# Delta layer: the neighbours' bias written to its scratch during the inverse, two square sums behind tile six, the eighth square sum and its copy one tile later

## The chip, the cores and the metric

The kernel runs on one core of a Trainium2 chip. The metric is the device time of one execution in microseconds. The kernel before takes 2214.55 us, the median of three runs.

The engines are called by their roles here: TensorE (PE in the profile) multiplies matrices, VectorE (DVE) and ScalarE (ACT) work element by element, GpSimd (POOL) does a few element-wise steps and issues some transfers, SyncE (SP) issues most of the transfers. Each engine works through its own instructions in order, and the engines wait for one another by semaphores.

## What is computed

The reference runs two blocks of two layers each over 256 tokens of width 1024. The change lies in the very first layer, a gated delta rule:

```python
def gdn_mixer(x, w_in, conv_w, a_log, dt_bias, norm_w, w_o):
    proj = x @ w_in
    qkv = jax.nn.silu(causal_depthwise_conv(proj[..., :3 * hk], conv_w))
    q = l2_normalize(qkv[..., :hk].reshape(shp)) * (GDN_HEAD_DIM ** -0.5)
    k = l2_normalize(qkv[..., hk:2 * hk].reshape(shp))
    v = qkv[..., 2 * hk:3 * hk].reshape(shp)
    ...
    o = gated_delta_rule_chunked(q, k, v, g, beta)
    o = rms_norm(o, norm_w) * jax.nn.silu(z)
    return o.reshape(b, t, hk).astype(x.dtype) @ w_o
```

`l2_normalize` divides by the root of the sum of squares over each head's 128 columns, for 8 heads of q and 8 of k. `gated_delta_rule_chunked` solves with a unit lower triangular matrix per chunk and head; the kernel inverts it.

The neighbourhood attention of the second block adds a bias `rpb` to its scores, which depends on the distance of two grid cells. That bias is a small input (8 heads, 2 layers). The kernel spreads it into a scratch in device memory early on and reads it back in the second block, from 1070 us on.

## The kernel before

**The projection by tiles.** `gdn_layer` works on x (turned, so that channels lie on the partitions). The weight `gdn_w_in` comes in 16 panels of 1 MB through a ring of three buffers, loaded by SyncE (`load_panel`, line 433); the buffer of a panel is free for the third next one when the panel has been split. For each panel ScalarE makes a rounded high half (`lin.high`, line 2153) and VectorE the rest as a low half (`lin.low`, line 2166), and there are two buffers for the halves. A panel holds two tiles of 128 output columns, so there are 32 tiles (GDN_OUT). TensorE makes each tile of 24 products (lines 355 to 357: 8 parts of the sum by three products of halves) of 256 tokens, into PSUM banks 0 to 2 in turn. Tiles 0 to 7 are q, 8 to 15 k, 16 to 23 v, 24 to 31 the gate z.

**What follows a tile.** ScalarE copies tile t out with the last tap of the convolution (`evict`, line 2505), VectorE adds the other three taps from PSUM (`conv`, line 2668), ScalarE applies the silu (line 2511) and, for q and k, squares the result (line 2517) into one of four buffers. TensorE sums a square over the partitions by a product with a matrix of ones (`square_sum`, line 2373): sums 0 and 1 go to the halves of bank 3, 2 and 3 to bank 4, 4 and 5 to bank 3 and so on. ScalarE copies a pair of sums out (`sums_out`, line 2540).

**What sets the order.** Everything is written out by hand in each engine's block, in loops over t. In TensorE's loop, the list `summed_behind` says which square sums come behind which tile; without an entry it is sum t - 5 behind tile t. Sum 0 waits also for D_ROWS, which VectorE raises at the end of `rows()` (last instruction at line 2694), a step behind the convolution of tile 4 that reads banks 3 to 7 for the decay. In ScalarE's loop, silu and square of tile t - 2 stand behind `evict(t)`, except that at t = 9, 10, 11 the exponentials of the decay stand there, and at t = 12, 13, 14 two silus with their squares. Square t (from 4 on) waits for sum t - 4, whose buffer it takes. A sum with an even number from 4 on waits for the copy of the pair before the last. In ScalarE's loop `sums_out` of pair p stands at t = 2p + 7. The high halves of the next panel are made at the start of `evict(t)` for even t, as soon as tile t - 1 has been multiplied; the low halves stand in VectorE's loop ahead of `conv(t)` for even t. In VectorE's loop two masks of the decay follow `conv(6)` and `conv(8)`.

**GpSimd.** It clears `pad` (line 2299), loads the neighbours' bias into it by 16 small transfers (line 2057), waits for them, and issues two transfers (line 2061) that write each layer's rows 64 times over into `rpb_dram`, 1792 KB each. Later it multiplies by beta, and during the inverse it makes the left factors of the products: `pair[lev % 2][t]` for levels 1 to 5 and the two chunks t (line 2316), each 128x1024. Its last instruction in the layer is the wait for the two stores.

**The inverse.** Six levels (LEVELS). At each level and for each chunk TensorE multiplies `pair` with X, ScalarE copies the product out, TensorE makes two more products, and VectorE subtracts them from X and its transpose (lines 2792 and 2794). TensorE waits for GpSimd's `pair` of the level by `ready`. In between VectorE also makes low halves of the output weight, behind level 1.

Of the kernel before, what the change touches and what calls it, by code (L numbers as in the profile page):

```python
# [42 lines left out]
ROWS = SEQ // GRID_W  # L43
# [2002 lines left out]
    dve_n.passed(6)  # L2046


def store_rpb(pr, pool, pad):


    i = pr.ins
    n_rows, at = 2 * ROWS - 1, GRID_W - WIN_COLS
    pool.wait_ge(pr.table_set.sem, pr.table_set.at(1))
    for l in range(DEPTH):
        for h in range(8):
            pool.dma_start(pad[h * n_rows:(h + 1) * n_rows, l, at:at + 2 * WIN_COLS - 1],
                           i["rpb_b_2"][l, h, WIN_ROWS - ROWS:WIN_ROWS + ROWS - 1, :]).then_inc(pr.rpb_in.sem, 16)
    pool.wait_ge(pr.rpb_in.sem, pr.rpb_in.at(16 * 8 * DEPTH))
    for l in range(DEPTH):  # L2060
        pool.dma_start(pr.rpb_dram[l].rearrange("c r x -> r c x"),
                       pad[:, l, :].unsqueeze(1).to_broadcast([8 * n_rows, GRID_W, P])).then_inc(pr.rpb_out.sem, 16)
# [145 lines left out]
def gdn_layer(pr, hand):  # L2208
# [12 lines left out]
    with ExitStack() as ctx:  # L2221
# [33 lines left out]
        pad = pr.sb(ctx, "rpb_rows", [8 * (2 * ROWS - 1), DEPTH, P])  # L2255
# [12 lines left out]
        with nc.Block() as block:  # L2268
# [27 lines left out]
            @block.gpsimd  # L2296
            def _(pool):
                pool.wait_ge(pr.taken_dve.sem, by_dve(0))
                pool.memset(pad[:, :, :], 0.0).then_inc(pr.table_set.sem, 1)
                store_rpb(pr, pool, pad)  # L2300

                pool.wait_ge(load.sem, load.at(80))
                pool.wait_ge(act_n.sem, act_n.at(A_DECAY))
                pool.wait_ge(pr.taken_dve.sem, by_dve(GDN_V + 1))
                for t in range(2):
                    pool.tensor_tensor(A[:, t], A[:, t], beta[:, t, :].unsqueeze(2).to_broadcast([P, H, P]), ALU.mult).then_inc(ready.sem, 1)
                for lev in range(1, LEVELS):
                    for t in range(2):
                        if lev == 1 and t == 0:
                            pool.wait_ge(ss_mm.sem, ss_mm.at(GDN_V))  # L2310
                        if lev == 1:
                            pool.wait_ge(dve_n.sem, dve_n.at(D_V))
                            pool.wait_ge(act_n.sem, act_n.at(A_AT + t))
                        else:
                            inv[t].begin(pool, 4 * (lev - 2) + 1)
                        pool.tensor_tensor(pair[lev % 2][t], AT[:, t], pr.const(f"pairT{2 << lev}").unsqueeze(1).to_broadcast([P, H, P]), ALU.mult).then_inc(ready.sem, 1)
                pool.wait_ge(pr.rpb_out.sem, pr.rpb_out.at(32))

            @block.tensor
            def _(pe):  # L2320
# [76 lines left out]
                            mm = pe.transpose(bank(K_BANKS[h // 4])[:, h % 4, :], k[:, h, chunk[0]], ident)  # L2397
                    mm.then_inc(pe_n.sem, 1)

                summed_behind = {12: [], 13: [7], 14: [8, 9], 15: [10, 11], 16: [12], 17: []}  # L2400
                pe.wait_ge(pr.ones_set.sem, pr.ones_set.at(2))
                for _ in range(10):
                    pe.matmul(ps[:, 2, 0:P], pr.full_ones, pr.full_ones, start=True, stop=True)
# [91 lines left out]
            def _(act):  # L2495
# [23 lines left out]
                def small():  # L2519
                    act.wait_ge(dve_n.sem, dve_n.at(D_LOGIT))  # L2520
                    act.activation(rate, par[:, 0, :], ACT.Exp)
                    act.activation(beta, ab[:, :, H:2 * H], ACT.Tanh, scale=0.5)
                    do(act.activation(soft, neg_abs, ACT.Exp))
                    act.activation(soft, soft, ACT.Ln, bias=1.0).then_inc(act_n.sem, 1)
# [13 lines left out]
                def sums_out(p):  # L2538
                    act.wait_ge(ss_mm.sem, ss_mm.at(2 * p + 2))
                    act.activation(sums[:, 2 * p:2 * p + 2, :].rearrange("p n c -> p (n c)"), ps[:, 3 + p % 2, :], ACT.Copy).then_inc(ss_out.sem, 1)  # L2540
# [29 lines left out]
                for t in range(GDN_OUT):  # L2570
                    evict(t)
                    if t == 0:
                        act.wait_ge(pe_n.sem, pe_n.at(P_AB))
                        act.activation(ab[:, :, :], ps[:, 3, 0:32].rearrange("p (t c) -> p t c", t=2), ACT.Copy).then_inc(act_n.sem, 1)
                        small()
                    if t in (9, 10, 11):
                        decay(t - 9)
                    elif t in (12, 13, 14):
                        silu(2 * t - 17)
                        silu(2 * t - 16)  # L2580
                    elif 2 <= t < 22:
                        silu(t - 2)
                    if t >= 7 and t % 2 and t <= 21:
                        sums_out((t - 7) // 2)
                    if t in (21, 22):
                        log(t - 21)
                    if t in (23, 25):
                        lin.high(act, lin.next_panel(t + 1))
                    if t in (23, 24):
                        root(t - 23)  # L2590
                    if t in (25, 26):
                        silu(2 * t - 30)
                        silu(2 * t - 29)
# [1506 lines left out]
```

## Time and profile before

| | us |
|---|---|
| runs of the kernel before | 2213.85, 2214.55, 2215.47 |
| median | 2214.55 |
| span of the profiled execution | 2222.0 |
| TensorE busy in it | 2150.3 |
| VectorE busy | 1610.9 |
| ScalarE busy | 1194.4 |
| GpSimd busy | 163.1 |

The span goes from the first to the last instruction of one profiled execution; it is 7.45 us longer than the median of the plain runs. A row of the timeline gives the start and the length of a group of like instructions in us, then engine, line, operation, what is written and read, the count, and in brackets how long the engine stood idle before it and what released it. Times count from the start of the span.

### The profile page before, as it was taken

Reading aid. Unit: us, or ns where it says so; the run is one execution under the profiler, and the core shown is the slowest. Engines: PE = TensorE matmul, PEld = TensorE weight load, DVE = VectorE, ACT = ScalarE, POOL = GpSimd, SP = SyncE. Lnnn points to the kernel's source line nnn. Section 1 sums busy time; section 2 is a strip of 40 time slices with the busy share of each in tenths; the row PEclk is TensorE's granted clock in tenths of the full one; section 3 lists DMA queues with packets and bytes.
Section 4 is the critical chain, followed back from the end, with each engine's and each line's share of the span. In section 5 each row is a group of like instructions: output and inputs, shape, how many; then the busy total and the mean of one; then the engine's idle time right before and its main releaser. Section 6 shows DMA issues by size and latency. Waiting matters only on the chain.

```text
span 2222.0 us, 39694 instructions
## 1 busy us (share of the span) xinstructions
PE 2150.3 (97%) x16153; PEld 1987.7 (89%) x16153; DVE 1610.9 (72%) x2318; ACT 1194.4 (54%) x1701; POOL 163.1 (7%) x182
## 2 busy tenths in 40 slices
PE   9999999999899998999999999999999999999998
PEld 8988788888678887999988999999999988899997
DVE  6775788855688887777767667777877876757664
ACT  5855577655667766333566545333433456545433
POOL 2140000002000000000510001000000410001000
PEclk9999999999999999999999999999999999999999
DMA  8522499874149993555632345555555653346552
GB/s 227 181 78 78 178 337 336 307 207 144 39 161 355 339 338 116 180 176 177 178 114 95 99 149 190 171 170 170 172 178 177 177 155 114 115 152 218 171 197 87
DMA packets 258570, 400.20 MB, mean 180 GB/s; under 512 B 17081, under 2 KB 204338, under 8 KB 258418
## 3 DMA queue, kind: packets, MB, share of 16 engines
q1 hardware_dynamic: 253138, 383.83, 51.4%
q0 software_dynamic: 5168, 14.17, 2.7%
q8 instruction: 111, 1.82, 0.3%
q14 instruction: 41, 0.34, 0.1%
q10 hardware_dynamic: 112, 0.05, 0.0%
HBM read 390.15 MB, written 7.86 MB: 179 GB/s over the span
## 4 chain that ended last, share of the span: by engine, by line
PE 52%; DVE 4%; ACT 2%; DMA 2%; issue 1%; DVEq 0%; ACTq 0%
PE psum_banks L355 15%; PE psum_banks L357 15%; PE psum_banks L356 15%; DMA weight_ring<-w_in 2%; DVE weights_low L780 1%; PE psum_banks L3538 1%; PE psum_banks L364 1%; PE psum_banks L365 1%; PE psum_banks L366 1%; ACT weights_high L2153 1%; PE psum_banks L3544 1%; PE psum_banks L3563 1%; DVE source_low L633 1%; PE psum_banks L3573 0%; PE psum_banks L3604 0%
## 5 line engine op out<-in xcount | busy, mean ns | idle before, releaser
L355 PE MATMUL psum_banks<-source_high,weights_high 128*128 128x272 f32 (+1 forms) x2336 | 680.5, 291 | 8.8 <-DVE hidden L795 3.7
L357 PE MATMUL psum_banks<-source_high,weights_low 128*128 128x272 f32 (+1 forms) x2336 | 671.0, 287 | 0.0
L356 PE MATMUL psum_banks<-source_low,weights_high 128*128 128x272 f32 (+1 forms) x2336 | 670.1, 287 | 0.0
L355 PEld LDWEIGHTS psum_banks<-source_high,weights_high 128*128 128x128 f32 x2336 | 442.2, 189 | 14.6 <-issue 7.2
L356 PEld LDWEIGHTS psum_banks<-source_low,weights_high 128*128 128x128 f32 x2336 | 442.6, 189 | 0.9
L357 PEld LDWEIGHTS psum_banks<-source_high,weights_low 128*128 128x128 f32 x2336 | 442.0, 189 | 0.0
L780 DVE TENSOR_TENSOR weights_low<-weight_ring,weights_high 128x2048 fp32r<-128x2048 f32 x131 | 293.1, 2290 | 94.9 <-ACT weights_high L774 94.8
L774 ACT ACTIVATE weights_high<-weight_ring 128x2048 fp32r<-128x2048 f32 x131 | 242.1, 1910 | 179.8 <-PE psum_banks L357 138.3
L2166 DVE TENSOR_TENSOR weights_low<-weight_ring,weights_high 128x2048 fp32r<-128x2048 f32 x96 | 223.0, 2323 | 145.1 <-ACT weights_high L2153 144.6
L2153 ACT ACTIVATE weights_high<-weight_ring 128x2048 fp32r<-128x2048 f32 x95 | 181.3, 1908 | 27.3 <-PE psum_banks L357 19.4
L785 ACT ACTIVATE silu_gate<-silu_gate 128x272 f32<-128x272 f32 (+1 forms) x88 | 37.7, 428 | 271.8 <-DVE silu_gate L794 271.8
L1804 DVE TENSOR_TENSOR weights_low<-weight_ring,weights_high 128x2048 fp32r<-128x2048 f32 x70 | 160.3, 2291 | 22.9 <-ACT weights_high L1581 22.4
L355 PE MATMUL psum_banks<-hidden_high,weights_high 128*128 128x272 f32 x528 | 153.3, 290 | 0.3 <-DVE h L808 0.3
L357 PE MATMUL psum_banks<-hidden_high,weights_low 128*128 128x272 f32 x528 | 152.4, 289 | 0.0
L356 PE MATMUL psum_banks<-hidden_low,weights_high 128*128 128x272 f32 x528 | 151.8, 287 | 0.0
L1581 ACT ACTIVATE weights_high<-weight_ring 128x2048 fp32r<-128x2048 f32 x70 | 133.7, 1914 | 26.6 <-PE psum_banks L366 21.4
L808 DVE SCALAR_TENSOR_TENSOR h<-psum_banks,h 128x272 f32<-128x272 f32 x264 | 107.8, 437 | 32.9 <-PE psum_banks L357 31.4
L1804 DVE TENSOR_TENSOR weights_low<-more_ring,weights_high 128x2048 fp32r<-128x2048 f32 x50 | 114.5, 2290 | 14.9 <-ACT weights_high L1581 14.6
L364 PE MATMUL psum_banks<-weights_high,hidden_high 128*128 128x512 f32 x256 | 102.2, 399 | 6.0 <-DVE weights_low L1804 2.7
L621 POOL TENSOR_TENSOR normed<-normed 128x272 f32<-128x272 f32 (+1 forms) x35 | 35.9, 1026 | 971.9 <-ACT normed L613 969.4
L1581 ACT ACTIVATE weights_high<-more_ring 128x2048 fp32r<-128x2048 f32 x50 | 95.6, 1912 | 19.0 <-PE psum_banks L366 17.5
L364 PE MATMUL psum_banks<-weights_high,slots 128*128 128x512 f32 (+1 forms) x256 | 99.3, 388 | 1.6 <-issue 0.9
(541 smaller groups left out, 4392.7 us busy)
## 6 DMA issues: line engine op xcount, KB each, us to landing
weight_ring<-ffn_w_in SPq DMA_DIRECT2D x88, 1024.0 KB, 6.7
weight_ring<-w_in SPq DMA_DIRECT2D x48, 1024.0 KB, 5.2
weight_ring<-ffn_w_out SPq DMA_DIRECT2D x44, 1024.0 KB, 5.0
weight_ring<-moe_w_down SPq DMA_DIRECT2D x24, 1024.0 KB, 6.6
weight_ring<-moe_w_gate SPq DMA_DIRECT2D x44, 512.0 KB, 4.8
weight_ring<-moe_w_up SPq DMA_DIRECT2D x44, 512.0 KB, 6.4
weight_ring<-gdn_w_in SPq DMA_DIRECT2D x16, 1024.0 KB, 6.0
more_ring<-moe_w_gate SPq DMA_DIRECT2D x32, 512.0 KB, 5.2
```

Source lines behind the costliest of these rows:

```text
L355: pe.matmul(out, w_hi, x_hi, start=start, stop=False)
L356: pe.matmul(out, w_hi, x_lo, start=False, stop=False)
L357: return pe.matmul(out, w_lo, x_hi, start=False, stop=stop)
L364: pe.matmul(out, x_hi, w_hi, start=start, stop=False)
L774: act.activation(split_at(par, part)[0], pr.ring[:, n % RING, :], ACT.Copy).then_inc(hi_n.sem, 1)
L780: dve.tensor_tensor(lo, pr.ring[:, n % RING, :], hi.bitcast(F32), ALU.subtract).then_inc(lo_n.sem, 1)
L785: act.activation(silu[:, m, toks], silu[:, m, toks], ACT.Silu).then_inc(sd.sem, 1)
L808: dve.scalar_tensor_tensor(h[:, j, toks], ps[:, 4 + j % 4, toks], 0.5, h[:, j, toks], ALU.mult, ALU.add).then_inc(ad.sem, 1)
L1581: act.activation(split_at(s)[0], ring_at(u, part), ACT.Copy).then_inc(hi_n.sem, 1)
L1804: dve.tensor_tensor(lo, ring_at(u, part), hi.bitcast(F32), ALU.subtract).then_inc(lo_n.sem, 1)
L2153: act.activation(self.hi[:, p % self.slots, :], self.pr.ring[:, n % RING, :], ACT.Copy).then_inc(self.pr.split_hi.sem, 1)
L2166: dve.tensor_tensor(self.lo[:, p % self.slots, :], self.pr.ring[:, n % RING, :], self.hi[:, p % self.slots, :].bitcast(F32), ALU.subtract) ...
```

## The change

The function that loads the neighbours' bias and writes it to its scratch is cut in two. The loads stay where they were. The wait for them and the two stores go into GpSimd's loop over the levels of the inverse, behind both chunks' products for level 2 and ahead of those for level 3. GpSimd's wait for the end of the stores stays the last of the layer.

In TensorE's list the square sums 0 and 1 both go behind tile 6 (they were behind tiles 5 and 6), and sum 7 goes behind tile 14 (it was behind 13), so that tile 14 is followed by sums 7, 8 and 9. In ScalarE's loop the copy of sums 6 and 7 goes from t = 13 to t = 14, behind the two silus and squares of that turn.

```diff
-def store_rpb(pr, pool, pad):
+def load_rpb(pr, pool, pad):
 
 
     i = pr.ins
@@ -2056,6 +2056,11 @@
         for h in range(8):
             pool.dma_start(pad[h * n_rows:(h + 1) * n_rows, l, at:at + 2 * WIN_COLS - 1],
                            i["rpb_b_2"][l, h, WIN_ROWS - ROWS:WIN_ROWS + ROWS - 1, :]).then_inc(pr.rpb_in.sem, 16)
+
+
+def store_rpb(pr, pool, pad):
+
+    n_rows = 2 * ROWS - 1
     pool.wait_ge(pr.rpb_in.sem, pr.rpb_in.at(16 * 8 * DEPTH))
     for l in range(DEPTH):
         pool.dma_start(pr.rpb_dram[l].rearrange("c r x -> r c x"),
@@ -2297,7 +2302,7 @@
                 pool.memset(pad[:, :, :], 0.0).then_inc(pr.table_set.sem, 1)
-                store_rpb(pr, pool, pad)
+                load_rpb(pr, pool, pad)
@@ -2314,6 +2319,8 @@
                         pool.tensor_tensor(pair[lev % 2][t], AT[:, t], pr.const(f"pairT{2 << lev}").unsqueeze(1).to_broadcast([P, H, P]), ALU.mult).then_inc(ready.sem, 1)
+                    if lev == 2:
+                        store_rpb(pr, pool, pad)
                 pool.wait_ge(pr.rpb_out.sem, pr.rpb_out.at(32))
@@ -2397,7 +2404,7 @@
-                summed_behind = {12: [], 13: [7], 14: [8, 9], 15: [10, 11], 16: [12], 17: []}
+                summed_behind = {5: [], 6: [0, 1], 12: [], 13: [], 14: [7, 8, 9], 15: [10, 11], 16: [12], 17: []}
@@ -2580,8 +2587,10 @@
-                    if t >= 7 and t % 2 and t <= 21:
+                    if t >= 7 and t % 2 and t <= 21 and t != 13:
                         sums_out((t - 7) // 2)
+                    if t == 14:
+                        sums_out(3)
```

## Rows read from the trace of the kernel before

**Rows 1.** The page, section 1: busy us, share of the span, instructions.

```profile
PE 2150.3 (97%) x16153; PEld 1987.7 (89%) x16153; DVE 1610.9 (72%) x2318; ACT 1194.4 (54%) x1701; POOL 163.1 (7%) x182
```

**Rows 2.** Waits of TensorE, 0 to 140 us: us in total, times, longest.

```profile
PE psum_banks L2373 <- DVE decay_small L2694: 2.5, 1, 2.5
PE psum_banks L355 <- DVE weights_low L2166: 2.2, 1, 2.2
...
PE psum_banks L2373 <- ACT squares L2517: 0.8, 1, 0.8
```

**Rows 3.** Timeline of TensorE: first products of tiles 6 and 7.

```profile
42.41 0.47 PE L355 MATMUL psum_banks<-slots,weights_high 128*128 128x256 f32 x1
...
45.71 0.47 PE L355 MATMUL psum_banks<-slots,weights_high 128*128 128x256 f32 x1
```

**Rows 4.** Timeline, 69 to 79 us: tiles 14 and 15, square 12, sums 10 and 11.

```profile
69.00 2.29 DVE L2166 TENSOR_TENSOR weights_low<-weight_ring,weights_high 128x2048 fp32r<-128x2048 f32 x1 [1.47 <-ACT weights_high L2153]
...
71.91 0.47 PE L355 MATMUL psum_banks<-slots,weights_high 128*128 128x256 f32 x1
...
75.64 0.47 PE L355 MATMUL psum_banks<-slots,weights_high 128*128 128x256 f32 x1
...
77.89 0.42 ACT L2517 ACTIVATE squares<-qkv 128x256 f32<-128x256 f32 x1
...
78.70 1.03 PE L2373 MATMUL psum_banks<-squares,full_ones 128*128 128x256 f32 x4
```

**Rows 5.** Windows: length, busy PE, PEld, DVE, ACT, POOL; clock, DMA share, GB/s.

```profile
74.90:140.00 65.10, 64.63 (x530) 63.48 (x529) 50.58 (x52) 43.50 (x60) 5.80 (x2) 1.00 0.43 137
```

**Rows 6.** Timeline, 46 to 56 us: VectorE ahead of tile 10, and tile 10.

```profile
46.18 1.52 DVE L2668 SCALAR_TENSOR_TENSOR qkv<-psum_banks,conv_w,qkv 128x253 f32<-128x253 f32 x3 [0.60 <-ACT qkv L2505]
...
49.81 1.51 DVE L2668 SCALAR_TENSOR_TENSOR qkv<-psum_banks,conv_w,qkv 128x253 f32<-128x253 f32 x3
52.52 2.29 DVE L2166 TENSOR_TENSOR weights_low<-weight_ring,weights_high 128x2048 fp32r<-128x2048 f32 x1 [1.20 <-ACT weights_high L2153]
...
55.61 0.47 PE L355 MATMUL psum_banks<-slots,weights_high 128*128 128x256 f32 x1
```

**Rows 7.** Line 2061, the two stores: ns min/median/max, first and last start.

```profile
L2061 POOL DMA_DIRECT2D rpb_scratch<-rpb_rows x2: 1680/1710/1741, 30.5 to 32.2; - x2
...
DMA to landing us min/median/max: 16.4/21.9/27.3
```

**Rows 8.** Line 433, the only weight load issued between 35 and 45.5 us.

```profile
L433 SPq DMA_DIRECT2D weight_ring<-gdn_w_in x1: 368/368/368, 35.2 to 35.2; - x1
...
DMA to landing us min/median/max: 25.2/25.2/25.2
```

**Rows 9.** Transfers issued from 0 to 230 us: KB each, median us to landing.

```profile
weight_ring<-gdn_w_in SPq DMA_DIRECT2D x16, 1024.0 KB, 6.0
```

**Rows 10.** Timeline, 60 to 65 us: halves for tile 12, and tile 12.

```profile
60.44 1.91 ACT L2153 ACTIVATE weights_high<-weight_ring 128x2048 fp32r<-128x2048 f32 x1 [1.36 <-DMA weight_ring<-gdn_w_in]
...
62.39 2.29 DVE L2166 TENSOR_TENSOR weights_low<-weight_ring,weights_high 128x2048 fp32r<-128x2048 f32 x1 [2.52 <-ACT weights_high L2153]
...
64.73 0.39 PE L355 MATMUL psum_banks<-slots,weights_high 128*128 128x256 f32 x1 [2.17 <-DVE weights_low L2166]
```

**Rows 11.** Timeline of the inverse, 153 to 177 us.

```profile
153.11 2.35 POOL L2316 TENSOR_TENSOR squares<-a_turned,consts_gdn 128x1024 f32<-128x1024 f32 x1
...
155.64 4.28 DVE L2166 TENSOR_TENSOR weights_low<-weight_ring,weights_high 128x2048 fp32r<-128x2048 f32 x1
...
161.53 1.15 PE L2425 MATMUL psum_banks<-inverse_pair,squares 64*64 64x64 f32 x32 [0.98 <-DVE inverse_pair L2794]
...
163.09 1.15 PE L2425 MATMUL psum_banks<-inverse_pair,spare_pair 64*64 64x64 f32 x32 [0.41 <-DVE inverse_pair L2794]
...
176.29 1.95 PE L2326 MATMUL psum_banks<-inverse_pair,spare_pair 128*128 128x128 f32 x16
```

**Rows 12.** The core: span, and mean granted clock of TensorE.

```profile
core 0: 2222.0 us, clock 0.990
```

## Prediction

> **What bounds the kernel now.** I began with the page's busy shares: TensorE is busy for 97% of the span [rows 1], so the time falls only where TensorE stands idle. The change touches the first 200 of 2222 us, so I went next to what TensorE waits for in the first 140 us. Three waits lie in the changed region: 2.5 us at a square sum (line 2373) for VectorE's line 2694, 2.2 us at a tile for the low halves of its weights (line 2166), and 0.8 us at a square sum for ScalarE's square (line 2517) [rows 2]. Then I read the order of time around each. A wait names only the engine that came last, so the reader must look there for what would have come next. The same rows give the unit prices: a tile of 24 products takes 3.30 us from its first product to that of the next tile when one square sum lies behind it (42.41 to 45.71 [rows 3]), and 3.73 us with two (71.91 to 75.64 [rows 4]). So one more sum costs 0.43 us, and a tile without any takes 2.87. From 74.9 to 140 us TensorE is busy for 64.63 of 65.10 us at the full clock [rows 5]: what is won before is carried through that stretch, and nothing is to be won in it. A difference under 0.2% (4.4 us) is about what a measurement of this kernel can't tell from no change.
>
> **Part 1, the first two sums behind tile 6.** Now sum 0 stands behind tile 5 and holds TensorE for 2.5 us [rows 2], because VectorE is still making the decay rows out of the banks that the sum overwrites; tile 6 starts at 42.41 [rows 3]. With the sum behind tile 6, tile 6 starts at once and ends near 42.5, when the decay rows are done. The two sums follow, the number of sums stays the same, and tile 7 stands at 45.71 - 2.5 = 43.2 us. ScalarE's square 4 needs sum 0 for its buffer, but it comes after the copy of tile 6, which is later than the sum: nothing. What is late next is VectorE's queue. It has 0.60 us of idle before the convolution at 46.18. Without that idle it starts this convolution at 45.58, needs 3.63 us to the start of the next (46.18 to 49.81, the mask lies between), 1.45 for that one, and begins the low halves for tile 10 at 50.66 where it began them at 52.52; they last 2.29 us, to 52.95 [rows 6]. Tile 10 stood at 55.61 [rows 6]; less 2.5 is 53.1. It just fits, with 0.15 us to spare. Part 1 gives 2.5 us; if VectorE's queue is longer by more than the spare, the excess is lost.
>
> **Part 2, the scratch written later.** The two stores of 1792 KB each start at 30.5 and 32.2 us and take 16.4 and 27.3 us to land [rows 7]. In that time SyncE issues the load of one weight panel at 35.2 us, which lands 25.2 us later, at 60.4 [rows 8]; the median of the 16 such loads is 6.0 us [rows 9]. ScalarE waits 1.36 us for it before the high halves at 60.44, the low halves follow at 62.39, and tile 12 starts at 64.73 after 2.17 us of idle [rows 10]. Without the wait ScalarE would come to it at 59.08, and with part 1 at 56.6. A load of 6 us from 35.2 is there at 41, with 15 us to spare. So the 1.36 us goes entirely and tile 12 stands at 64.73 - 2.5 - 1.36 = 60.87. The other 0.8 us of the idle stays: it is ScalarE's own queue (the exponentials of the decay stand in it). Part 2 gives 1.36 here, not 2.17.
>
> Where the stores go, GpSimd issues for 2 x 1.71 = 3.42 us [rows 7] after the second level's products, so its third-level products begin at 156.5 instead of 153.11 (times of before; all shifts alike) [rows 11]. Behind them are queued those of levels four and five, and TensorE waits for each. VectorE's low halves at 155.64 take 4.28 us, against 2.29 elsewhere [rows 6, 11]: they stood behind a GpSimd product. That makes VectorE late, and TensorE idles 0.98 us before 161.53 and 0.41 before 163.09 [rows 11]. With GpSimd busy issuing instead, VectorE starts at once and is done at 157.93; two third-level products of 2.35 us each [rows 11] then end at 160.3 and 162.6. TensorE starts the first at about 160.5 and the second at 162.7 instead of 163.09: a gain of 0.4 us, with GpSimd last. The next two pairs end at 167.3 and 172.0; TensorE came to the second half of level five at 176.29, so 6.6 us per level, and to that of level four near 169.7 [rows 11]: time to spare in both. Bounds for the inverse: 0.9 us gained, if GpSimd is never last, and 3.4 lost, if its whole issue time reaches TensorE. I take 0.4, where the rows put it. The landing is hidden: from 156.6 it may take 27.3 us again, to 184, and behind the product at 176.29 the rest of level five, the state products and the output part are still to come before GpSimd's last wait matters.
>
> The Trainium skill (SBUF — State Buffer, "SBUF: two separate sides") says that VectorE and GpSimd share one port pair as an exclusive lock, held by the first to start for its whole instruction; a VectorE instruction with two SBUF inputs takes part in it against a GpSimd one that reads SBUF. By that rule, the trace agrees: 4.28 us [rows 11]. The same section warns that GpSimd can't write a transfer's descriptors while VectorE holds the pair in its faster modes; applied to these low halves the second issue would stretch to the end of them, which is the first price of rival C.
>
> **Part 3, the eighth sum and its copy a tile later.** Sum 7 waits 0.8 us behind tile 13 [rows 2], but tile 14 needs low halves that are made from 69.00 for 2.29 us. It could have started at 71.34 where it started at 71.91 [rows 4]. So the wait is worth 0.57 us only, and one sum goes behind tile 14 for 0.43. Tile 14 stands 3.86 + 0.57 = 4.4 us sooner, tile 15 only 4.4 - 0.43 = 4.0: net 0.1. The copy (line 2540) now comes behind square 12, and sum 10 must await it, as it overwrites the same bank. Square 12 starts at 77.89 and lasts 0.42; ScalarE comes to it 3.86 + 0.48 us sooner (the copy no longer lies ahead), so it ends at 73.97 and the copy, 0.6 at most, by 74.55. Sum 10 stood at 78.70 [rows 4]; less 4.0 is 74.7. It fits, again by 0.15 us. Bounds 0 and 0.6 us, the copy's length; I take 0.
>
> **The sum.** 2.5 + 1.36 + 0.1 + 0.4 = 4.4 us. The profiled execution's span is 2222.0 us, 7.45 over the median of the runs. The stretches in question run at full clock and nothing in them would scale the difference, so 4.4 comes off both: 2217.6 for the span, 2214.55 - 4.4 = 2210.2 for the median. Behind the layer nothing is changed. The mean granted clock of 0.990 [rows 12] says that some short stretches run at 1.2 GHz; a shift of 4 us may add or remove part of one. I bound this at 1.5 us either way, an estimate.
>
> **Rivals.** A, the forecast: 2210.2 (2209.0 to 2211.3), chance 0.58. B, a thin margin fails: VectorE's queue at tile 10 or the copy ahead of sum 10 comes late. For it: both margins are 0.15 us, and a semaphore between two engines takes a part of that. Against it: the queues are back to back in the rows already. Price 0.6 to 1.9 us, so 2210.8 to 2212.1; chance 0.16. C, GpSimd's issues become the wait in the inverse. It is last already in my sum. If VectorE's low halves hold the second issue to 157.93, the pair ends at 161.2 and 163.6, 0.9 us worse than A; if the whole 3.42 reaches TensorE, 3.8 worse: 2211.1 to 2214.0, chance 0.12. Against it: the two issues of now lasted 1.68 and 1.74 us [rows 7], though such low halves ran beside the second. D, slower than before: the stores now fill the transfer engines while TensorE runs the inverse, hundreds of products in few us, whose instructions must themselves be loaded by transfers. If one such load is held as the panel was, 25.2 against 6.0, so by up to 19 us [rows 8, 9], the kernel is slower by over 0.2% from the point where 8.8 us of it meet TensorE: 2219 to 2229. Against it: the same stores lay beside tiles 3 to 10, and there no wait of TensorE is without a named releaser [rows 2]. Chance 0.05. E, more than the forecast: the 0.8 us before tile 12 and all of the inverse's 0.9 fall too, or a slow clock stretch goes: 2206.5 to 2209, chance 0.09. That the change does nothing would need the load at 35.2 to be late for another reason and VectorE to stay last at tile 7; the rows leave no room for both.
>
> **How the numbers follow.** The line at 0.2% is 2214.55 - 4.43 = 2210.1, in the middle of A. 0.37 of A lies below it; with E that is 0.46 for faster. The rest of A, B and C make 0.49 for the same, D 0.05 for slower. The range goes from inside E, 2207.3, to 2213.0, most of C; what it leaves out is D and the ends of C and E.
>
> **What would show it.** Right: no wait at line 2373 before 80 us; the load near 35 us lands in under 10; one wait of 0.8 us at tile 12; the low halves in the inverse last 2.3 us; tile 15 stands 4.0 us sooner. Wrong: a wait for line 2166 at tile 10, for line 2540 behind tile 15, for GpSimd's line 2316 well over 0.1 us, or TensorE idle with no releaser while the stores land.

## The result, and the profile after

The changed kernel takes 2230.31 us (median of 11 runs, 2225.66 to 2237.27), where the kernel before takes 2217.77 beside it (11 runs, 2213.85 to 2228.44; the three known before the prediction were among the lowest). The ratio is 1.0054, with a 95% interval from 1.0041 to 1.0067: about 12 us slower, where 4.4 us less were forecast. The profiled execution has a span of 2226.9 us, 4.9 more than before.

First, the waits of TensorE from 0 to 140 us, as in [rows 2] (us in total, times, longest):

```profile
PE psum_banks L2410 <- DVE full_ones L2742: 1.9, 1, 1.9
PE psum_banks L355 <- DVE weights_low L2171: 1.3, 2, 0.7
PE psum_banks L2432 <- issue: 0.4, 1, 0.4
```

Both waits at the square sums are gone (line 2373 is 2380 now). The low halves (2166, now 2171) are waited for twice: 0.7 us at tile 12 and 0.6 at tile 14. The weight load issued near 35 us lands in 6 us, against the 25.2 of [rows 8]:

```profile
L433 SPq DMA_DIRECT2D weight_ring<-gdn_w_in x1: 368/368/368, 36.1 to 36.1; - x1
...
DMA to landing us min/median/max: 6.1/6.1/6.1
```

So far it went as written. The waits of TensorE from 130 to 200 us show where the time went:

```profile
PE psum_banks L2432 <- DVE inverse_pair L2803: 8.4, 4, 6.8
PE psum_banks L2432 <- issue: 4.6, 2, 4.3
```

In the kernel before, the first was 3.5 us in total, with none over 1.0, and the second 0.4. A wait that the profile puts down to "issue" is one without a named releaser. The timeline of the inverse, which answers to [rows 11], shows both in their places (start, length, engine, line, what, idle before):

```profile
149.56 3.48 POOL L2066 DMA_DIRECT2D rpb_scratch<-rpb_rows  x2
...
152.11 10.07 DVE L2171 TENSOR_TENSOR weights_low<-weight_ring,weights_high 128x2048 fp32r<-128x2048 f32 x1
...
153.03 2.40 POOL L2321 TENSOR_TENSOR squares<-a_turned,consts_gdn 128x1024 f32<-128x1024 f32 x1
...
155.35 2.38 POOL L2321 TENSOR_TENSOR spare_pair<-a_turned,consts_gdn 128x1024 f32<-128x1024 f32 x1
...
157.66 6.72 POOL L2321 TENSOR_TENSOR temp<-a_turned,consts_gdn 128x1024 f32<-128x1024 f32 x2
...
163.79 1.97 PE L2432 MATMUL psum_banks<-inverse_pair,squares 64*64 64x64 f32 x32 [6.78 <-DVE inverse_pair L2803]
...
173.96 0.26 PE L2432 MATMUL psum_banks<-inverse_pair,a_strict 64*64 64x64 f32 x1 [4.25 <-issue]
```

VectorE's low halves last 10.07 us. They are asked for at 152.11, while GpSimd issues, and end at 162.18. GpSimd's products go ahead of them: two of 2.4 us, untouched, and one of the next pair. The fourth waits for VectorE. Until then VectorE can't subtract level 2, and TensorE idles 6.78 us. At 169.7 TensorE stops again, for 4.25 us in the middle of a group of 32 equal products, and no engine is named. And the clock falls. The windows (length, busy PE, PEld, DVE, ACT, POOL, then granted clock, DMA share, GB/s):

```profile
158.00:162.00 4.00, 0.00 (x0) 0.00 (x0) 4.00 (x1) 0.00 (x0) 4.00 (x2) 0.92 1.00 190
162.00:166.00 4.00, 2.21 (x42) 2.21 (x44) 3.20 (x9) 0.13 (x1) 2.52 (x2) 0.50 0.98 177
166.00:170.00 4.00, 3.71 (x91) 3.57 (x89) 0.00 (x0) 1.92 (x2) 4.00 (x2) 0.73 0.88 164
170.00:174.00 4.00, 0.04 (x2) 0.04 (x2) 0.00 (x0) 0.00 (x0) 0.52 (x1) 0.70 0.93 207
174.00:178.00 4.00, 4.00 (x77) 4.00 (x78) 1.82 (x5) 0.00 (x0) 0.00 (x0) 0.50 0.55 165
```

With each of the two stops the clock goes to 0.50, its 1.2 GHz level, for a while, and 32 products take about 1.7 us instead of 0.93. The transfer engines are 88 to 100% busy from 158 to 174 us.

The first product behind the inverse (line 2453, now 2460) is the mark by which all runs can be compared. It starts at 182.69 us in the kernel before and here at

```profile
192.50 2.02 PE L2460 MATMUL psum_banks<-v_tokens,inverse_pair 128*128 128x128 f32 x16 [0.87 <-DVE inverse_pair L2807]
```

which is 9.8 us later. But 0.9 us of that arose ahead of everything that was changed. From 16 to 25 us TensorE works without a pause in every trace. In most of them part of that stretch is at the 1.2 GHz level, and how much differs between executions of the same code. The windows (columns as above) of the kernel before, of the changed kernel, and of the run below in which SyncE issues the stores:

```profile
16.00:25.00 9.00, 9.00 (x64) 8.82 (x65) 4.91 (x9) 3.93 (x10) 4.81 (x10) 0.81 0.78 244
```

```profile
16.00:25.00 9.00, 9.00 (x51) 8.68 (x51) 3.85 (x8) 2.83 (x8) 5.45 (x11) 0.62 0.77 238
```

```profile
16.00:25.00 9.00, 9.00 (x76) 8.83 (x76) 6.33 (x17) 4.29 (x8) 5.27 (x11) 1.00 0.76 240
```

So the mark alone can be off by up to 3 us, and what a change did is better read from ScalarE's copy of tile 4 on, which stands ahead of the first moved sum. It starts at 36.72 us in the kernel before and at 37.63 here:

```profile
36.72 0.47 ACT L2505 ACTIVATE qkv<-psum_banks,conv_w 128x256 f32<-128x256 f32 x1 [3.86 <-PE psum_banks L357]
```

```profile
37.63 0.47 ACT L2512 ACTIVATE qkv<-psum_banks,conv_w 128x256 f32<-128x256 f32 x1 [3.87 <-PE psum_banks L357]
```

From there to the transposes that open the last stage before the inverse (135.11 us before, 131.58 here) it takes 94.0 us instead of 98.4, and from the transposes to the mark 60.9 instead of 47.6. So the tiles gained 4.4 us and the inverse lost about 13: 4.9 more of waits put down to VectorE, 4.2 more of waits that name nobody, and the rest, about 4, by the slow clock.

### The profile page after: what moved, and what is told of

Its sections match the earlier page's. It is cut to its first block, busy times and chain, and to the rows that moved or that the text cites. A ratio compares the mean times of both kernels' runs of the same rounds, so it can differ in the third digit from the quotient of the medians.

```text
span 2226.9 us, 39694 instructions
## 1 busy us (share of the span) xinstructions
PE 2151.9 (97%) x16153; PEld 1989.8 (89%) x16153; DVE 1615.4 (73%) x2318; ACT 1194.3 (54%) x1701; POOL 165.0 (7%) x182
## 4 chain that ended last, share of the span: by engine, by line
PE 52%; DVE 4%; ACT 2%; DMA 1%; issue 1%; DVEq 0%; ACTq 0%
PE psum_banks L355 15%; PE psum_banks L357 14%; PE psum_banks L356 14%; DMA weight_ring<-w_in 1%; DVE weights_low L780 1%; PE psum_banks L3547 1%; PE psum_banks L364 1%; PE psum_banks L365 1%; PE psum_banks L366 1%; ACT weights_high L2158 1%; PE psum_banks L3553 1%; PE psum_banks L3572 1%; DVE source_low L633 1%; PE psum_banks L3582 0%; PE psum_banks L3613 0%
## 5 line engine op out<-in xcount | busy, mean ns | idle before, releaser
L356 PE MATMUL psum_banks<-hidden_low,weights_high 128*128 128x272 f32 x528 | 151.7, 287 | 0.0
```

The lines of the kernel that those rows point to most:

```text
L356: pe.matmul(out, w_hi, x_lo, start=False, stop=False)
```

## Two theories and the experiments

Both began from the two stops. LOCK: GpSimd's issue, and its products behind it, shut VectorE out while its low halves read two inputs from SBUF. LOAD: the 3.67 MB of the stores fill the transfer engines, and TensorE's own instructions, which come by transfers, arrive late. The rival to both is that the moved square sums did the harm. In what follows "mark" is the start of the first product behind the inverse (before 182.69, after 192.50). Behind it stands, as "from tile 4", the time from the copy of tile 4 to the mark (before 146.0, after 154.9), which is free of what happens at 16 to 25 us. Each trace is of one execution. Each ratio is that to the kernel before, run beside it on the same chip.

### The moved sums alone

```diff
                 load_rpb(pr, pool, pad)
+                store_rpb(pr, pool, pad)
 ...
-                    if lev == 2:
-                        store_rpb(pr, pool, pad)
```

> The changed kernel with the stores back at the start of the layer, so that only the moves of the square sums and of the copy remain. If the loss lies in the inverse (both theories below say so), the inverse is as in the kernel before: low halves there about 4.3 us, no TensorE wait without a releaser in it. The wait of 2.5 us at the first square sum and the 0.8 us one are gone; the wait for the late weight panel at tile 12 stays or grows to about 4.5 us, since its landing near 60 us doesn't move. Total 0 to 3 us under the kernel before (ratio 0.9986 to 1.0000). If the moved sums were themselves the loss, it would be slower than the kernel before by 5 us or more.

Measured: ratio 1.0005 (0.9991 to 1.0018). The mark is at 182.31, from tile 4 it is 146.0 us, as before. Waits of TensorE:

```profile
PE psum_banks L355 <- DVE weights_low L2171: 4.6, 1, 4.6
PE psum_banks L2431 <- DVE inverse_pair L2802: 3.5, 5, 1.0
```

The 2.5 us of the first sum turn up again at tile 12, where the wait grew from 2.2 to 4.6 us, because the late panel lands near 60 us whatever TensorE does. So the sums did no harm, and alone they bring nothing.

### The stores alone

```diff
-                summed_behind = {5: [], 6: [0, 1], 12: [], 13: [], 14: [7, 8, 9], 15: [10, 11], 16: [12], 17: []}
+                summed_behind = {12: [], 13: [7], 14: [8, 9], 15: [10, 11], 16: [12], 17: []}
 ...
-                    if t >= 7 and t % 2 and t <= 21 and t != 13:
+                    if t >= 7 and t % 2 and t <= 21:
                         sums_out((t - 7) // 2)
-                    if t == 14:
-                        sums_out(3)
```

> The kernel before with only the stores moved into the inverse. If the stores' new place is the whole loss: low halves of 10 us again, TensorE idle 6 to 7 us for them, a wait without a releaser of about 4 us, TensorE's clock at half speed there; 1.36 us won at tile 12. Total 10 to 15 us over the kernel before (ratio 1.0045 to 1.007). If the loss needs both moves (the sums shift the inverse so that two things collide), the ratio is under 1.002.

Measured: ratio 1.0061 (1.0038 to 1.0084), mark at 195.72, from tile 4 157.8.

```profile
155.34 10.07 DVE L2171 TENSOR_TENSOR weights_low<-weight_ring,weights_high 128x2048 fp32r<-128x2048 f32 x1
...
167.02 1.97 PE L2432 MATMUL psum_banks<-inverse_pair,squares 64*64 64x64 f32 x32 [6.77 <-DVE inverse_pair L2801]
...
177.46 0.21 PE L2432 MATMUL psum_banks<-inverse_pair,a_strict 64*64 64x64 f32 x1 [4.57 <-issue]
```

The whole loss is here, 10.07 us to the digit. It belongs to the stores' place and to nothing else.

### Without VectorE's low halves in the inverse (LOCK taken away)

```diff
-                    if lev == 1:
-                        lin.low(dve, lin.next_panel(GDN_OUT - 2))
 ...
+                lin.low(dve, lin.next_panel(GDN_OUT - 2))
                 lin.low(dve, 17)
```

> The changed kernel with VectorE's low halves of the first output panel moved from behind level 1 to behind the last level, so that no VectorE instruction with two SBUF inputs stands beside GpSimd's issue. Theory LOCK (GpSimd's issue and products shut VectorE out, that is the loss): the 6.8 us idle of TensorE before level 3 goes, so does the fall of the clock behind it; total 8 to 14 us faster than the changed kernel, ratio to the kernel before 0.998 to 1.001. Theory LOAD (the stores fill the transfer engines and TensorE's instructions come late): the wait without a releaser of 4 us or more stays somewhere between 150 and 176 us and the clock falls behind it; ratio 1.002 to 1.005.

Measured: ratio 1.0027 (1.0012 to 1.0042), mark at 190.37, from tile 4 155.5.

```profile
PE psum_banks L2432 <- issue: 12.5, 3, 6.4
...
PE psum_banks L2432 <- DVE inverse_pair L2803: 1.4, 2, 0.7
```

The wait for VectorE is gone, 8.4 to 1.4 us. But from tile 4 to the mark nothing is won in this execution (155.5 against 154.9), as the waits that name nobody rise from 4.6 to 12.5. TensorE stands for 6.4 us before the same product as in the changed kernel, the first of level 3, now without a named releaser, and later for 5.7 us before the same last product of a group. The clock falls as before, to 0.50 from 158 to 162 us. The twelve runs are kinder (1.0027, where the changed kernel had 1.0054); the one profiled, 2233.32 us, was the second slowest of them. So the low halves can't be the only cause of the first stop: behind them stood another that lasted nearly as long.

### The stores issued by SyncE

```diff
+                while pr.loaded < 19:
+                    panel()
+                sp.wait_ge(ready.sem, ready.at(6))
+                store_rpb(pr, sp, pad)
                 load_ahead(pr, sp)
 ...
-                    if lev == 2:
-                        store_rpb(pr, pool, pad)
```

> The changed kernel with the two stores issued by SyncE instead of GpSimd, at the same moment (behind level 2's products of GpSimd). GpSimd issues nothing in the inverse. Theory LOCK: VectorE's low halves are back at 2.3 to 4.3 us, the 6.8 us idle goes, ratio to the kernel before 0.998 to 1.001 (unless the stores' landing holds TensorE by itself). Theory LOAD: the same bytes go at the same time, so the wait without a releaser stays, 4 us or more, with the clock's fall: ratio 1.002 to 1.005.

Measured: ratio 1.0034 (1.0020 to 1.0047), mark at 184.65, from tile 4 149.8. The execution that was profiled was the fastest of twelve (2216.31, their median is 2227.66), so its loss may be on the small side.

```profile
149.34 4.28 DVE L2171 TENSOR_TENSOR weights_low<-weight_ring,weights_high 128x2048 fp32r<-128x2048 f32 x1
...
157.67 1.97 PE L2434 MATMUL psum_banks<-inverse_pair,squares 64*64 64x64 f32 x32 [3.42 <-issue]
...
171.21 0.26 PE L2434 MATMUL psum_banks<-inverse_pair,temp 64*64 64x64 f32 x1 [2.25 <-issue]
```

With GpSimd issuing nothing, the low halves take the 4.28 us of the kernel before [rows 11]. So it is GpSimd's issue that shuts VectorE out, and not the bytes. The same bytes sent by another queue still stop TensorE, 6.0 us in all. Both theories hold.

What TensorE lacks in such a stop can be read from the transfers. The profile lists packets of a kind of their own, `instruction`, 16 KB each, and on queue q8 one of them starts every 4 to 5 us in the inverse of the kernel before: at 143.0, 147.9, 152.2, 157.0, 161.0 and 166.0 us. In the changed kernel none starts between 148.6 and 161.0, nor between that one and 171.6. All that the queues moved from 149 to 161 us (packets, MB, share of the 16 engines' time), before and after:

```profile
q8 instruction: 2, 0.03, 1.1%
```

```profile
q0 software_dynamic: 475, 1.67, 72.2%
```

Each long stop that names nobody ends 2.2 to 2.4 us after such a packet starts:

| run | packet starts | TensorE goes on |
|---|---|---|
| changed kernel | 171.6 | 173.96 |
| stores alone | 175.3 | 177.46 |
| low halves late | 158.5, 169.3 | 160.68, 171.70 |
| stores by SyncE | 155.4, 168.8 | 157.67, 171.21 |

A packet takes about 1 us once it has started, with the stores as without; it starts late. The profile doesn't say whose these packets are; that they carry TensorE's instructions follows from these times. Nor are they late because TensorE stands: with the low halves late one starts at 146.1 and the next is due near 150.6, while TensorE works on until 154.3. So LOAD is right: the instructions come late behind the stores' bytes. It holds for the first stop of the changed kernel too. There the packet starts at 161.0, so TensorE could have gone on at about 163.3 (an estimate from the table); VectorE let it go at 163.79, and the profile names only who came last.

### One eighth of the bytes in the inverse

`store_rpb` gets a range of the 64 copies as arguments:

```diff
+                store_rpb(pr, pool, pad, 8, GRID_W)
 ...
-                        store_rpb(pr, pool, pad)
+                        store_rpb(pr, pool, pad, 0, 8)
```

> The changed kernel with seven eighths of each store back at the start of the layer and one eighth (224 KB each) left behind level 2. Theory LOAD (the bytes in the inverse hold TensorE's instructions): transfers in the inverse last 3 us instead of 27, so the waits without a releaser shrink from 4 to 12 us to under 1. Theory LOCK (VectorE that asks for its second input while GpSimd issues is passed over): the issue is shorter (two of 0.5 to 1.7 us), and unless it still lies under the start of the low halves they fall from 10.1 to 4.3 us. Total within 0.1% of the run with the sums alone (ratio 0.999 to 1.002); the wait at tile 12 for the late panel is back.

Measured: ratio 1.0017 (1.0002 to 1.0032), mark at 186.31, from tile 4 148.5.

```profile
149.72 1.46 POOL L2066 DMA_DIRECT2D rpb_scratch<-rpb_rows  x2
151.21 2.36 POOL L2322 TENSOR_TENSOR squares<-a_turned,consts_gdn 128x1024 f32<-128x1024 f32 x1
152.27 10.36 DVE L2171 TENSOR_TENSOR weights_low<-weight_ring,weights_high 128x2048 fp32r<-128x2048 f32 x1
...
153.52 2.37 POOL L2322 TENSOR_TENSOR spare_pair<-a_turned,consts_gdn 128x1024 f32<-128x1024 f32 x1
155.84 4.64 POOL L2322 TENSOR_TENSOR temp<-a_turned,consts_gdn 128x1024 f32<-128x1024 f32 x2
```

```profile
PE psum_banks L2433 <- issue: 0.4, 1, 0.4
```

The waits that name nobody are back at the 0.4 us of the kernel before: LOAD is a matter of bytes. LOCK isn't, and it costs 7.0 us by itself: from the transposes to the mark it is 54.6 us here, 47.6 before. LOAD by itself cost 8.3 (55.8 with SyncE's stores), both together 13.3. The issue was over at 151.2, a microsecond before VectorE asked, and yet VectorE waited behind all four products, until GpSimd had nothing more to do at 160.5, and lasted 10.36 us. My expectation of 4.3 us for this case was wrong: VectorE is passed over after the issue too. Two expectations failed here in part: the wait at tile 12 didn't come back to its old size either (0.7 us, as in the changed kernel: with an eighth of the bytes gone from the start, the panel was in time).

### The stores behind GpSimd's last product

```diff
-                    if lev == 2:
-                        store_rpb(pr, pool, pad)
+                store_rpb(pr, pool, pad)
                 pool.wait_ge(pr.rpb_out.sem, pr.rpb_out.at(32))
```

> The changed kernel with both stores behind GpSimd's products for level 5, its last. LOCK: nothing of GpSimd comes behind the issue, and the low halves behind level 1 are made long before, so they take 4.3 us. LOAD: the stores land over the last levels and the state products, and the waits without a releaser move there, 4 to 8 us in all, with a fall of the clock. Ratio to the kernel before 1.000 to 1.004; if LOAD is wrong, 0.998.

Measured: ratio 0.9988 (0.9971 to 1.0006), mark at 179.59, from tile 4 141.6, 4.4 less than before. Low halves 4.29 us, waits that name nobody 0.4 us in all. The stores are issued at 165.9 and the last lands near 194; TensorE shows no stop in that time. I had expected 4 to 8 us of them. The instruction packets are 9 to 13 us apart there too, but TensorE starts only some 8 products per us from 174 to 190 us, where it started over 30. So the stores' bytes hurt TensorE's instructions where it runs through hundreds of 64x64 products, and not in the level of full products and the state part behind it.

### The stores beside the tiles

```diff
                     pool.tensor_tensor(A[:, t], A[:, t], beta[:, t, :].unsqueeze(2).to_broadcast([P, H, P]), ALU.mult).then_inc(ready.sem, 1)
+                store_rpb(pr, pool, pad)
 ...
-                    if lev == 2:
-                        store_rpb(pr, pool, pad)
```

> The changed kernel with both stores behind GpSimd's multiplication by beta, at about 91 us, beside tiles 18 to 24. LOAD: TensorE takes eight to nine instructions per us there against 25 in the inverse, so no wait without a releaser. Weight panels take up to 25 us to land again; TensorE waits up to 5 us for one. The inverse is as in the kernel before. Ratio 0.998 to 1.001.

Measured: ratio 1.0033 (1.0016 to 1.0050), mark at 189.58, from tile 4 151.7; the inverse is as before.

```profile
PE psum_banks L355 <- DVE weights_low L2171: 10.0, 3, 8.7
```

No stop without a name, as expected, but one of 8.7 us for a weight panel, where I had allowed 5. This is the old trouble of [rows 8] with less slack: beside these tiles too the stores cost more than they would save.

### The stores once the norms of q are made

```diff
+                pool.wait_ge(act_n.sem, act_n.at(A_NORM_Q))
+                store_rpb(pr, pool, pad)
```

(behind GpSimd's multiplication by beta, instead of in the inverse)

> The changed kernel with both stores issued once ScalarE has made the norms of q (about 108 us), where the panels loading are those of the output weight, needed 40 us later. LOCK and LOAD both say that it costs nothing there: no wait without a releaser, low halves in the inverse 4.3 us, no wait for a panel. The won 3.5 us at tile 15 are kept: ratio to the kernel before 0.997 to 0.9995, 3 to 4 us faster, and the best of all variants.

Measured: ratio 0.9980 (0.9966 to 0.9994), mark at 178.07, from tile 4 141.6, 4.4 less than before.

```profile
106.92 3.48 POOL L2066 DMA_DIRECT2D rpb_scratch<-rpb_rows  x2 [17.60 <-ACT inverse_pair L2557]
...
151.03 4.28 DVE L2171 TENSOR_TENSOR weights_low<-weight_ring,weights_high 128x2048 fp32r<-128x2048 f32 x1
```

All as expected, but for being the best of all: the next run came out lower still, and from tile 4 on the stores behind GpSimd's last product are as good as this. The stores land by 135.3 us, beside panels that are needed only from 147 us on, and ahead of the inverse.

### The same, with GpSimd only waiting at level 2

```diff
                         pool.tensor_tensor(pair[lev % 2][t], AT[:, t], ...).then_inc(ready.sem, 1)
+                    if lev == 2:
+                        inv[1].begin(pool, 9)
```

> Stores at the norms as in e8_store_norm; where the changed kernel issued them, GpSimd now only waits, for TensorE's first product of level 2 with the second chunk, 3 to 4 us later. GpSimd is then late as in the changed kernel but holds nothing. The step of the prediction under test: low halves 2.3 us, level 3's products of GpSimd from about 152, TensorE's second product of level 3 gains 0.2 to 0.9 us against e8. If instead GpSimd's lateness alone shuts VectorE out: low halves about 10 us, TensorE idle 6 to 7 us. Ratio to the kernel before 0.997 to 0.9995 in the first case, 1.000 to 1.003 in the second.

Measured: ratio 0.9971 (0.9955 to 0.9988), mark at 175.86, from tile 4 141.1.

```profile
149.29 2.29 DVE L2171 TENSOR_TENSOR weights_low<-weight_ring,weights_high 128x2048 fp32r<-128x2048 f32 x1
...
150.56 3.25 POOL L2323 TENSOR_TENSOR squares<-a_turned,consts_gdn 128x1024 f32<-128x1024 f32 x1 [3.76 <-PE psum_banks L2434]
153.76 2.35 POOL L2323 TENSOR_TENSOR spare_pair<-a_turned,consts_gdn 128x1024 f32<-128x1024 f32 x1
...
156.26 1.15 PE L2434 MATMUL psum_banks<-inverse_pair,spare_pair 64*64 64x64 f32 x32 [1.13 <-POOL spare_pair L2323]
```

This is what the prediction described for the inverse: GpSimd 3.8 us late, VectorE in at once and done in 2.29 us, GpSimd's second product of level 3 the last to come. That step was right for a GpSimd that is idle, and false for one that issues transfers. From the transposes to the mark it is 47.1 us, 0.5 less than before, where the prediction had 0.4. (The mark itself is 2.2 us sooner than with the stores at the norms alone, but 1.7 of that arose ahead of tile 4.) Its ratio is the lowest of all runs, though its interval overlaps that of the kernel without the wait; the interval leaves out 1, so against the kernel before it is faster, by about 0.3%.

### The same, with one more product of GpSimd at level 2

```diff
+                    if lev == 2:
+                        pool.wait_ge(pr.rpb_out.sem, pr.rpb_out.at(32))
+                        pool.tensor_tensor(extra[:, :, :], AT[:, 0], pr.const("pairT4")..., ALU.mult)
```

(the product goes into a new tile that nobody reads; the stores are at the norms of q)

> Stores at the norms as in e8_store_norm; where the changed kernel issued them, GpSimd makes one more product of 2.35 us into a tile that nobody reads (work added), so that VectorE asks for its low halves in the middle of GpSimd's first product of level 3, as in e5_eighth_store, but with no transfer issued before. If the shutting out comes from the issued transfer: low halves 4.3 to 4.8 us. If it comes from the place at which VectorE asks (GpSimd's next product is queued already): about 10 us, TensorE idle 6 to 7 us, ratio 1.001 to 1.004.

Measured: ratio 0.9980 (0.9965 to 0.9994), mark at 176.45, from tile 4 141.5.

```profile
149.17 2.36 POOL L2324 TENSOR_TENSOR squares<-a_turned,consts_gdn 128x1024 f32<-128x1024 f32 x1
149.40 4.28 DVE L2171 TENSOR_TENSOR weights_low<-weight_ring,weights_high 128x2048 fp32r<-128x2048 f32 x1
151.48 4.41 POOL L2324 TENSOR_TENSOR spare_pair<-a_turned,consts_gdn 128x1024 f32<-128x1024 f32 x1
```

VectorE asks while GpSimd makes its first product of level 3, as in the run with one eighth of the bytes, waits for that one only, and the next product waits for VectorE. So neither the place at which it asks nor GpSimd's lateness shuts VectorE out. What differs between 4.28 and 10.36 us is that GpSimd had issued a transfer just before. How an issue that is over keeps VectorE out behind the following products, no run here shows; it stays open. Against the run with the bare wait, TensorE comes to the second group of products of level 3 0.58 us later (156.84 against 156.26), 0.12 of it from ahead of tile 4.

### The stores at the norms, with the old sums

```diff
-                summed_behind = {5: [], 6: [0, 1], 12: [], 13: [], 14: [7, 8, 9], 15: [10, 11], 16: [12], 17: []}
+                summed_behind = {12: [], 13: [7], 14: [8, 9], 15: [10, 11], 16: [12], 17: []}
```

(and the copy back at t = 13)

> The kernel before with only the stores moved, to the norms of q. The wait for the panel at tile 12 goes (1.4 us), the waits at the first and the eighth square sum stay (2.5 and 0.8 us), the inverse is as before. TensorE stands 1.3 to 1.5 us sooner in the inverse than in the kernel before, against 3.5 to 4 us in e8_store_norm. Ratio 0.998 to 1.001. So the moved sums bring their 2 us only once the panel is no longer late.

Measured: ratio 1.0005 (0.9986 to 1.0023), mark at 180.87, from tile 4 144.5, 1.5 less than before. The sums' own waits are there (2.5 and 0.8 us). So from tile 4 on, the sums alone win nothing, the stores alone 1.5 us, and both moves 4.4. All runs together, in us (before the inverse: from the copy of tile 4 to the transposes; the inverse: from there to the mark):

| run | before the inverse | the inverse |
|---|---|---|
| kernel before | 98.4 | 47.6 |
| changed kernel | 94.0 | 60.9 |
| sums alone | 98.4 | 47.6 |
| stores alone | 96.9 | 60.9 |
| low halves late | 94.0 | 61.6 |
| stores by SyncE | 94.0 | 55.8 |
| one eighth in the inverse | 94.0 | 54.6 |
| stores behind the last product | 94.0 | 47.6 |
| stores beside the tiles | 104.1 | 47.6 |
| stores at the norms | 94.0 | 47.6 |
| the same with a wait | 94.0 | 47.1 |
| the same with a product | 94.0 | 47.6 |
| stores at the norms, old sums | 96.9 | 47.6 |

## Why the prediction was wrong

- **Unit prices and bound**: right. TensorE was carried through the tiles without a new stop.
- **Part 1**, 2.5 us: right, with a condition that the sum hid. The wait is gone and tile 10 isn't late, so VectorE's queue fits. But the gain exists only together with part 2 (alone 0.0 us from tile 4 on). I had added the two as if each stood for itself.
- **Part 2, the panel**, 1.36 us: right. The load lands in 6.1 us, and the wait left at tile 12 is 0.7 us where I said 0.8.
- **Part 3**, 0.1 us: right in size (0.2). The three parts gave 4.4 us ahead of the inverse where the sum had 3.96. Tile 14 waits for its low halves for 0.6 us, and no wait for the copy appears behind tile 15.
- **The inverse**, +0.4 us: this is the term that failed. It came out as about -13 us (60.9 against 47.6). Two sentences were false. "With GpSimd busy issuing instead, VectorE starts at once" rested on one issue of the kernel before that ran beside low halves without harm [rows 7]; there no product of GpSimd stood behind the issue. With an extra product or a bare wait in place of the issue the low halves took 4.28 and 2.29 us, so GpSimd's lateness alone is harmless, and with the wait the inverse did gain 0.5 us. "The landing is hidden" looked only for who waits for the stores, which is nobody, and not for who else uses the transfer engines at that moment. The second mechanism I had named, as rival D, with a chance of 0.05: the instructions of TensorE held up by the stores' bytes, which the instruction packets show. The first was in no rival. C had GpSimd late behind VectorE, where VectorE was shut out behind GpSimd. The two came together, with the slow clock as a third part that neither price held. My bound of 3.4 us lost for GpSimd's side was its issue time. The measured price was VectorE's wait behind the products that GpSimd had queued behind the issue: three of four in the changed kernel, until 159.9 us, and all four in the run with one eighth of the bytes.
- **The slow clock stretches**, which I bounded at 1.5 us either way: no row gave that number, and it was too small. What differs ahead of the change, mostly at 16 to 25 us, moved the copy of tile 4 by up to 3.2 us between traces (34.8 to 38.0).
- **The lock.** The rule that I cited from the Trainium skill (SBUF — State Buffer, "SBUF: two separate sides") explains a part of the first stop: VectorE with two SBUF inputs is blocked for whole instructions of GpSimd. Who starts first gets the pair, says the rule, and 4.28 us in the runs without an issue agrees. The 10.36 us doesn't follow from it, since VectorE was waiting when the second, third and fourth product started.
- **The argument against D** was that the same stores had lain beside tiles 3 to 10 without a stop. The rows were true, but the place wasn't comparable: there TensorE starts some 8 products per us, and in the inverse over 30. From 75 to 140 us of the kernel before 4 instruction packets start on q8, one in 16 us; in the inverse it is one in 4 to 5.
- The runs against which I set the median were low ones: 2214.55 then, 2217.77 with eight more. That shifts the forecast by 3 us and changes nothing in its sign.

## What to carry to other kernels

A transfer that nobody waits for still has a price where it lies: look at what else needs the transfer engines then, the instructions of an engine in a stretch of hundreds of tiny products above all. On GpSimd, keep issues away from the front of queued products when VectorE has an urgent instruction with two SBUF inputs beside them; a pause or another product in the same place cost nothing here. And where two stalls lie one behind the other, one edit alone may show nothing: take both away in one trial before dropping either. Where two causes of one stop end close together, the profile names only the later; its waits don't add up to what each would cost alone.

## What the runs showed of the hardware

The same code varies from execution to execution with the granted clock: the 26 runs of the kernel before that stood beside the last experiments took from 2213.47 us (mean granted clock 0.994) to 2225.90 (0.988). It shows in the traces too. Behind the mark the run with SyncE's stores and that with the stores at the norms run the same instructions of TensorE:

```profile
core 0: 2214.5 us, clock 0.992
```

```profile
core 0: 2217.5 us, clock 0.989
```

Behind their marks (184.65 and 178.07) they have 2029.9 and 2039.4 us. That is 9.5 us of difference, more than the whole change was to bring. For the same reason the span of the profile after is only 4.9 us over that of before while its mark is 9.8 us later. The spans of one profile each don't settle a change of 0.2% here. The ratio of many runs does, and inside a trace the time between two instructions that enclose the change, started behind the slow stretch at 16 to 25 us.

Two things more. The stores' bytes delay TensorE's own instruction packets: 12.4 and 10.6 us between two starts in the changed kernel, 4 to 5 in the kernel before. And a transfer issued by GpSimd keeps a VectorE instruction with two SBUF inputs waiting behind the GpSimd products that follow, 10.07 and 10.36 us instead of 4.28; why, no run here shows.
